# Two 64-column weight tiles in place of one 128-column tile in the experts' up projections

## The chip, the cores and the metric
The kernel runs on one core of one Trainium2 chip. The metric is the device time of one execution in microseconds (us). Three runs of the kernel before took 1402.24, 1405.08 and 1405.54 us; their median, 1405.08 us, is the number to compare with. Durations of single instructions come from one profiled execution.

## The reference, cut to what matters
The program is one inference step of a decoder layer: a mixer of a recurrent and a convolution group, a cross-attention, and a mixture of 64 experts, for 512 prompt tokens and 8 decoding tokens, all in float32. Only the experts matter here. Each token goes to 8 of 64 experts; expert e computes, for the rows x that chose it:

```
hb = jax.nn.silu(xb @ w1_e[e]) * (xb @ w3_e[e])     # (rows, 1024) @ (1024, 256), twice: the up projections
return (hb @ w2_e[e]) * g[:, None]                  # (rows, 256) @ (256, 1024), times the gate: down
```

The up projections of one expert are thus a product of 1024 input features with 512 output features (256 of w1_e, 256 of w3_e).

## The kernel before, in words
The last stage before the final sums is a loop over the 64 experts. Every expert has room for 112 rows (CAP). Five engines work on it at once, each with its own instruction order written out by hand and with semaphores between them:

- SyncE loads the three weight matrices of an expert (1 MB each) into one of four buffers in SBUF, `arena` in the profile.
- GpSimd gathers the 112 rows of x2 that the expert needs (L564), and scatters its 112 result rows (L570), both by indirect DMAs.
- TensorE does, for one expert after another, four things: `find` (5 small bfloat16 matmuls, 6 columns wide, that look up which rows belong to the expert), `turn_rows` (8 transposes of the gathered rows, L666), `up` (the up projections) and `down` (4 matmuls 512 wide). All matmuls are issued by the helper `mm` at L651, the transposes by `turn` at L666.
- ScalarE copies the transposed rows to `xgT` (L1347), takes the silu of the first half of the up result (L1351) and scales half of the down result (L1354).
- VectorE multiplies silu with the second half (L1817), scales the other half of the down result (L1820), and works out the next indices (L1803 to L1814).

In one step of TensorE's order the pieces stand as `up` of expert e, `turn_rows` of e + 1, `down` of e - 1, `find` of e + 3. So no piece needs the result of the one just ahead of it.

`up` (L1019 to L1027) holds the change. Four blocks j of 128 output features each (two of w1_e, two of w3_e) take 8 steps k of 128 input features. The weight tile, 128 x 128, is the stationary operand, the 112 gathered rows are the moving one, and the result goes to all 128 partitions of bank group 2 of PSUM, columns `at` to `at + 112`. That is 32 calls of `mm` for an expert. A call with float32 operands shows in the trace as two weight loads (LDWEIGHTS, the rows of engine PEld) and two MATMULs (engine PE), so `up` shows 64 of each. Two narrow uses of TensorE elsewhere are of interest: the router (`router`, 64 output features, at partition 0) and the transposes of decoding rows (8 partitions deep).

Of the kernel before, what the change touches and what calls it, by code (L numbers as in the profile page):

```python
# [14 lines left out]
P = 128  # L15
D = 1024
KC = D // P
# [12 lines left out]
CAP = 112  # L30
# [68 lines left out]
def decoder_step(nc: bass.Bass, ins, outs):  # L99
# [3 lines left out]
    with ExitStack() as ctx:  # L103
# [27 lines left out]
        psum = ctx.enter_context(nc.psum_tensor("psum", [P, 4, D], F32))  # L131
# [55 lines left out]
        xgT = act_mem[:, 2048:2048 + 2 * KC * CAP].rearrange("p (b k s) -> p b k s", b=2, k=KC)  # L187
# [37 lines left out]
        def value_cache(b):  # L225
            return cache(0, b) if b < 4 else cache(2, b - 4)
# [7 lines left out]
        def ew(n):  # L234

            at = 6144 * n
            return (arena[:, at:at + 4096].rearrange("p (w k n) -> p w k n", w=2, k=KC),
                    arena[:, at + 4096:at + 6144].rearrange("p (k n) -> p k n", k=2))
# [404 lines left out]
        def _(pe):  # L643
# [6 lines left out]
            def mm(out, lhsT, rhs, first, last):  # L650
                return pe.matmul(out, lhsT, rhs, start=first, stop=last)  # L651
# [12 lines left out]
            def turn(out, in_, n=P):  # L664

                return pe.transpose(out, in_, ident[0:n, 0:n])  # L666
# [3 lines left out]
            for c in range(KC):  # L670
                ps = open_group(f"x{c}")
                for t in range(TT):
                    w = width(t)
                    last = turn(ps[:, t * P:t * P + w], x_tok[0:w, t, c * P:(c + 1) * P], w)
# [38 lines left out]
            for j in range(2 * RC):  # L713
                name = ("zu", "zg")[j // RC] + str(j % RC)
                at = (j + RC) % (2 * RC)
# [3 lines left out]
            for g in range(2):  # L719
                ps = open_group(f"mt{g}")  # L720
                for c in range(4):
                    for m in range(2):
                        last = turn(ps[:, 256 * c + P * m:256 * c + P * m + P], mem_tok[:, m, (4 * g + c) * P:(4 * g + c + 1) * P])
# [20 lines left out]
            for c in range(RC):  # L744
                last = turn(ps[0:38, 512 + c * P:512 + (c + 1) * P], gluT[:, c, T - 38:T])
# [28 lines left out]
            for g in range(2):  # L774
                ps = open_group(f"kt{g}")
                for c in range(4):
                    for m in range(2):
                        last = turn(ps[:, 256 * c + P * m:256 * c + P * m + P], k_tok[:, m, (4 * g + c) * P:(4 * g + c + 1) * P])
# [3 lines left out]
            for c in range(RC):  # L782
                last = turn(ps[0:9, c * P:(c + 1) * P], ucT[:, c, SEQ - 1:T])
# [36 lines left out]
            for c in range(KC):  # L820
                last = turn(ps[0:NS, c * P:(c + 1) * P], qT[:, c, SEQ:T])
# [87 lines left out]
            for b in range(NS):  # L909
# [3 lines left out]
                for n in range(2):  # L913
                    last = mm(ps[0:NS, 512 * n:512 * n + 512], unit[:, NS * b:NS * b + NS],
                              value_cache(b)[:, 0, 512 * n:512 * n + 512], b == 0, b == NS - 1)
# [3 lines left out]
            for j in range(KC):  # L919
                last = turn(ps[:, NS * j:NS * j + NS], o_s[:, j * P:(j + 1) * P], NS)  # L920
# [41 lines left out]
            for t in range(TT):  # L962
                w = width(t)
                last = turn(ps[0:w, E * t:E * t + E], score_t[:, t * P:t * P + w], E)
# [11 lines left out]
            for t in range(TT):  # L976
                for u in range(t + 1):
                    last = mm(ps[:, E * t:E * t + E], tri if u == t else ones[:, :], sel_b[:, u, :], u == 0, u == t)
            last.then_inc(s_full, 1)
            ps = open_group("count")  # L980
            for t in range(TT):
                last = mm(ps[:, 0:E], ones[:, :], sel_b[:, t, :], t == 0, t == TT - 1)
# [36 lines left out]
            def up(b, part):  # L1019

                wu, _ = ew(part)
                for j in range(4):
                    at = 512 * b + CAP * j
                    for k in range(KC):
                        last = mm(psum[:, 2, at:at + CAP], wu[:, j // 2, k, P * (j % 2):P * (j % 2) + P], xgT[:, b, k, :],
                                  k == 0, k == KC - 1)
                return last  # L1027

            def down(b, part):
# [19 lines left out]
            def c_step(e, n, wait_w):  # L1049
                pe.wait_ge(m_xc, e + 1)  # L1050
                pe.wait_ge(s_w[n % 4], wait_w)
                if at_least(e, 2):
                    pe.wait_ge(m_hd, e - 1)
                up(n % 2, n % 4).then_inc(m_h, 1)
# [42 lines left out]
            with pe.If(n_max > CAP):  # L1097
                pe.wait_ge(m_ya, E)
                pe.wait_ge(m_yv, E)
                with pe.Fori(0, E * (ROUNDS - 1)) as i:  # L1100
                    pe.wait_ge(f_sem["oh"], i + 1)
                    find(0, i % E).then_inc(f_sem["ip"], 1)
                    pe.wait_ge(f_sem["g"], 16 * i + 16)
                    turn_rows(0).then_inc(f_sem["xt"], 1)
                    pe.wait_ge(f_sem["xc"], i + 1)
                    pe.wait_ge(f_sem["w"], 48 * i + 48)
                    up(0, 0).then_inc(f_sem["h"], 1)
                    pe.wait_ge(f_sem["hd"], i + 1)
                    down(0, 0).then_inc(f_sem["y"], 1)
# [4 lines left out]
            for n, t in enumerate(LAST_ORDER):  # L1114
# [5 lines left out]
                for q in range(3):  # L1120
                    pe.wait_ge(s_yin[q][n % 3], 16 * (n // 3 + 1))
                    for j in PE_ROWS[q]:
                        for h in range(2):
                            last = mm(psum[0:w, n % 4, 512 * h:512 * h + 512], ident[0:w, 0:w],
                                      y_in[n % 3][0:w, j, 512 * h:512 * h + 512], j == 2, j == 5)
# [836 lines left out]
```

## Time and profile before

| | |
|---|---|
| median of the three runs | 1405.08 us (1402.24 to 1405.54) |
| profiled execution, first to last instruction (the span) | 1401.5 us, 19230 instructions |
| time around the span, taken as median less span | 3.6 us |
| granted TensorE clock, mean of the span | 0.969 of full speed |
| TensorE busy: MATMUL / weight loads | 92% / 72% of the span |
| VectorE, ScalarE, GpSimd busy | 35%, 20%, 16% |
| HBM traffic | 245 GB/s over the span |

The page gives the profiled execution by its span; the runs' time is 0.7 to 4.0 us above that span, and the difference of the medians is used. In the lists "PE" is the MATMUL and "PEld" the weight load, which can run while a MATMUL runs. "128\*64 128x260" means a stationary tile of 128 rows and 64 columns with a moving operand of 128 x 260. The duration of a MATMUL or a weight load holds its way through the pipeline; what it costs in a row of its kind is the distance from one start to the next, which is read from the timeline.

### The profile page before, as it was taken

How to read it: one execution, taken by the hardware profiler on the slowest of the kernel's cores; microseconds unless marked ns; L12 is line 12 of the kernel's file. 1: busy time of each engine (PE TensorE's matmuls, PEld its weight loads, DVE VectorE, ACT ScalarE, POOL GpSimd, SP SyncE). 2: the span in 40 equal slices, each digit the busy share in tenths (PEclk: the TensorE clock that was granted, in tenths of full speed). 3: DMA queues.
4: the chain of work that ended last, by engine and by line, in shares of the span. 5: the costliest groups of instructions: out<-in, count | busy, mean ns of one | idle time of the engine just before them, and what ended most of it. 6: DMA issues, size and time to landing. Idle time of an engine off the chain costs nothing.

```text
span 1401.5 us, 19230 instructions
## 1 busy us (share of the span) xinstructions
PE 1282.4 (92%) x7579; PEld 1009.6 (72%) x7579; DVE 495.9 (35%) x1063; ACT 275.4 (20%) x454; POOL 226.2 (16%) x212
## 2 busy tenths in 40 slices
PE   5999596999979999999999999999999999999651
PEld 4888254868846685788888888888888888888420
DVE  0169998131187348111111111111111111111078
ACT  1125124022235150111111111111111111111100
POOL 2039000000000002011111111111111111111061
PEclk9999798999999999999999999999999999999887
DMA  9330303033155532688888888888888888888193
GB/s 340 152 120 2 134 11 150 1 120 136 59 190 233 181 139 69 246 312 318 321 312 313 315 313 310 306 311 308 312 314 315 312 316 311 308 309 305 41 381 160
DMA packets 75990, 319.12 MB, mean 228 GB/s; under 512 B 14055, under 2 KB 20415, under 8 KB 55941
## 3 DMA queue, kind: packets, MB, share of 16 engines
q1 hardware_dynamic: 57525, 278.60, 53.3%
q0 software_dynamic: 16992, 35.49, 7.0%
q10 hardware_dynamic: 1424, 4.35, 0.8%
q8 instruction: 34, 0.56, 0.2%
q14 instruction: 15, 0.12, 0.0%
HBM read 307.16 MB, written 36.38 MB: 245 GB/s over the span
## 4 chain that ended last, share of the span: by engine, by line
PE 77%; DVE 17%; DMA 2%; issue 1%; ACT 1%; POOL 0%; ACTq 0%; DVEq 0%; POOLq 0%; SPq 0%
PE psum L651 73%; DVE act_mem L1461 7%; PE psum L666 5%; DVE act_mem L1921 2%; DMA act_mem<-in_w_conv_b_dram 1%; DVE mk_mem L1621 1%; DVE act_mem L1529 1%; DVE st L1927 1%; DVE act_mem L1932 0%; DMA arena<-in_w_o_dram 0%; DVE act_mem L1915 0%; DVE act_mem L1559 0%; DVE act_mem L1475 0%; DMA arena<-y_rows 0%; DMA y_rows<-act_mem,idx_y 0%
## 5 line engine op out<-in xcount | busy, mean ns | idle before, releaser
L651 PE MATMUL psum<-act_mem,arena 128*128 128x112 f32 (+1 forms) x5504 | 791.6, 305 | 6.7 <-DMA arena<-in_w_o_dram 3.8
L651 PEld LDWEIGHTS psum<-act_mem,arena 128*128 128x128 f32 x5504 | 736.0, 193 | 52.6 <-DMA arena<-in_w_o_dram 4.6
L651 PE MATMUL psum<-arena,act_mem 128*112 128x512 f32 (+2 forms) x616 | 276.7, 593 | 1.0 <-DVE act_mem L1820 0.9
L651 PEld LDWEIGHTS psum<-arena,act_mem 128*112 128x112 f32 (+2 forms) x616 | 101.5, 174 | 124.5 <-issue 123.7
L570 POOL DMA_INDIRECT y_rows<-act_mem,idx_y x64 | 72.6, 1134 | 616.5 <-DVE idx_x L1814 580.4
L1817 DVE TENSOR_TENSOR act_mem<-act_mem,psum 128x224 f32<-128x224 f32 x64 | 24.8, 388 | 389.9 <-ACT act_mem L1351 389.9
L1820 DVE TENSOR_SCALAR act_mem<-psum,act_mem 112x512 f32<-112x512 f32 x64 | 48.0, 750 | 227.9 <-PE psum L651 227.9
L1351 ACT ACTIVATE act_mem<-psum 128x224 f32<-128x224 f32 x64 | 22.9, 358 | 433.3 <-PE psum L651 433.3
L1461 DVE SCALAR_TENSOR_TENSOR act_mem<-act_mem,wcb 128x511 f32<-128x511 f32 (+29 forms) x90 | 86.9, 1016 | 1.1
L1354 ACT ACTIVATE act_mem<-psum,act_mem 112x512 f32<-112x512 f32 x64 | 44.0, 687 | 164.6 <-PE psum L651 164.6
L666 PE MATMUL psum<-ident,act_mem 112*128 112x112 f32 (+4 forms) x390 | 53.5, 280 | 24.8 <-DMA act_mem<-in_x_sample_dram 10.0
L1347 ACT ACTIVATE act_mem<-psum 128x896 f32<-128x896 f32 x64 | 58.7, 917 | 60.8 <-PE psum L666 60.8
L666 PEld LDWEIGHTS psum<-ident,act_mem 112*128 112x128 f32 (+4 forms) x390 | 46.1, 179 | 30.6 <-issue 17.5
L651 PE MATMUL psum<-arena,ident 128*128 128x512 f32 x48 | 26.0, 677 | 31.4 <-DMA arena<-y_rows 31.4
L651 PEld LDWEIGHTS psum<-act_mem 128*112 128x112 bf16 x320 | 26.4, 131 | 34.7 <-issue 34.7
L1803 DVE TENSOR_TENSOR act_mem<-act_mem,gate_w 128x560 bf16<-128x560 f32 x64 | 47.3, 740 | 0.0
L526 POOL TENSOR_TENSOR act_mem<-act_mem,kv_mem 128x511 f32<-128x511 f32 (+29 forms) x30 | 44.0, 1467 | 11.4 <-ACT kv_mem L1160 9.5
L651 PEld LDWEIGHTS psum<-arena,ident 128*128 128x128 f32 x48 | 9.4, 212 | 48.0 <-issue 30.6
L651 PE MATMUL psum<-arena,kv_mem 128*128 128x512 f32 x96 | 41.8, 593 | 1.2 <-ACT kv_mem L1176 1.2
L666 PE MATMUL psum<-ident,mk_mem 112*128 112x112 f32 (+5 forms) x316 | 40.1, 269 | 1.1 <-ACT mk_mem L1314 1.1
L666 PEld LDWEIGHTS psum<-ident,mk_mem 112*128 112x128 f32 (+5 forms) x316 | 36.9, 189 | 3.3 <-ACT mk_mem L1314 2.0
L564 POOL DMA_INDIRECT act_mem<-x_rows,idx_x x32 | 32.2, 1005 | 16.3 <-issue 9.5
(221 smaller groups left out, 705.9 us busy)
## 6 DMA issues: line engine op xcount, KB each, us to landing
arena<-in_w_e_dram SPq DMA_DIRECT2D x192, 1024.0 KB, 7.9
arena<-in_w_in_dram SPq DMA_DIRECT2D x16, 512.0 KB, 16.9
arena<-in_cache_mem_k_dram SPq DMA_DIRECT2D x8, 1024.0 KB, 9.1
arena<-in_cache_mem_v_dram SPq DMA_DIRECT2D x8, 1024.0 KB, 11.6
arena<-y_rows SPq DMA_DIRECT2D x8, 1024.0 KB, 12.8
arena<-y_rows SPq DMA_DIRECT2D x4, 1536.0 KB, 8.7
arena<-in_w_v_dram SPq DMA_DIRECT2D x1, 4096.0 KB, 24.3
arena<-in_w_k_dram SPq DMA_DIRECT2D x1, 4096.0 KB, 14.0
```

The costliest lines, as they stand in the source:

```text
L526: gp.tensor_tensor(out[:, n:SEQ], out[:, n:SEQ], tap_mem[:, product % 4, 0:SEQ - n], ALU.add).then_inc(s_convp, 1)
L564: gp.indirect_dma_start(out=xg[b][0:CAP, :], out_offset=None, in_=x2_rows[:, :], in_offset=bass.IndirectOffsetOnAxis(ap=idx_x[0:CAP, n:n + ...
L570: gp.indirect_dma_start(out=y_rows[:, :], out_offset=bass.IndirectOffsetOnAxis(ap=idx_y[0:CAP, n:n + 1], axis=0), in_=ys[0:CAP, b, :], in_ ...
L651: return pe.matmul(out, lhsT, rhs, start=first, stop=last)
L666: return pe.transpose(out, in_, ident[0:n, 0:n])
L1347: return act.activation(xgT[:, b, :, :].rearrange("p (h k) s -> p h (k s)", h=2), psum[:, 1, :].rearrange("p (h n) -> p h n", h=2)[:, :, 0 ...
L1354: return act.activation(ys[0:CAP, b, 0:512], psum[0:CAP, 0, 0:512], ACT.Copy, scale=picked[0:CAP, n, 1:2])
L1461: return dve.scalar_tensor_tensor(out, in0, w, in1, ALU.mult, ALU.add)
L1803: return dve.tensor_tensor(onehot[:, n % 2, :, :], place[:, :, bass.ds(e, 1)].broadcast_to([P, TT, CAP]), numbers.unsqueeze(1).broadcast_t ...
L1817: return dve.tensor_tensor(hidT[:, b, :], silu[:, b, :], psum[:, 2, 512 * b + 2 * CAP:512 * b + 4 * CAP], ALU.mult)
L1820: return dve.tensor_scalar(ys[0:CAP, b, 512:1024], psum[0:CAP, 0, 512:1024], picked[0:CAP, n, 1:2], None, ALU.mult)
L1921: ins = dve.tensor_tensor(x, x, y_in[m % 3][0:w, j, :], ALU.add)
```

## The change
Each of the 32 calls of `mm` in `up` becomes two. The first takes the lower 64 columns of the weight tile and writes partitions 0 to 63 of the same PSUM columns, the second takes the upper 64 columns and writes partitions 64 to 127. Both have the same moving operand. Nothing else in the kernel is touched; the semaphores, the buffers and the order of the pieces stay.

```diff
                 for j in range(4):
                     at = 512 * b + CAP * j
                     for k in range(KC):
-                        last = mm(psum[:, 2, at:at + CAP], wu[:, j // 2, k, P * (j % 2):P * (j % 2) + P], xgT[:, b, k, :],
-                                  k == 0, k == KC - 1)
+                        for h in range(2):
+                            f = P * (j % 2) + 64 * h
+                            last = mm(psum[64 * h:64 * h + 64, 2, at:at + CAP], wu[:, j // 2, k, f:f + 64], xgT[:, b, k, :],
+                                      k == 0, k == KC - 1)
                 return last
```

The first place is TensorE's order where the expert loop starts: the rows "128x112" from `act_mem` and `arena` are `up`, those of L666 `turn_rows`, "112x512" is `down`, "112x6" is `find`. Before:

```order
L666 MATMUL psum<-ident,act_mem 128x112 x8
L651 MATMUL psum<-act_mem,arena 128x112 x32
L666 MATMUL psum<-ident,act_mem 128x112 x8
L651 MATMUL psum<-act_mem,arena 128x112 x32
L666 MATMUL psum<-ident,mk_mem 128x112 x8
L651 MATMUL psum<-arena,act_mem 112x512 x4
L651 MATMUL psum<-act_mem 112x6 x5
```

And the same place now:

```order
L666 MATMUL psum<-ident,act_mem 128x112 x8
L651 MATMUL psum<-act_mem,arena 64x112 x64
L666 MATMUL psum<-ident,act_mem 128x112 x8
L651 MATMUL psum<-act_mem,arena 64x112 x64
L666 MATMUL psum<-ident,mk_mem 128x112 x8
L651 MATMUL psum<-arena,act_mem 112x512 x4
L651 MATMUL psum<-act_mem 112x6 x5
```

Each `up` has 64 calls of 64 output partitions where it had 32 of 128; the pieces ahead of it and behind it, which are 112 or 128 columns wide, stand where they stood. The calls alternate between the lower and the upper partitions. The other engines' orders are the same but for line numbers.

## Rows read from the trace of the kernel before

**Rows 1.** The page: busy time of each engine, and the chain that ended last.
```profile
PE 1282.4 (92%) x7579; PEld 1009.6 (72%) x7579; DVE 495.9 (35%) x1063; ACT 275.4 (20%) x454; POOL 226.2 (16%) x212
...
PE psum L651 73%; DVE act_mem L1461 7%; PE psum L666 5%; DVE act_mem L1921 2%; DMA act_mem<-in_w_conv_b_dram 1%; DVE mk_mem L1621 1%; DVE act_mem L1529 1%; DVE st L1927 1%; DVE act_mem L1932 0%; DMA arena<-in_w_o_dram 0%; DVE act_mem L1915 0%; DVE act_mem L1559 0%; DVE act_mem L1475 0%; DMA arena<-y_rows 0%; DMA y_rows<-act_mem,idx_y 0%
```

**Rows 2.** Busy time by stretch of the expert loop; last: granted clock, DMA share, GB/s.
```profile
700.00:800.00 100.00, 100.00 (x713) 81.39 (x713) 18.16 (x49) 16.97 (x26) 17.25 (x16) 1.00 0.85 314
...
1000.00:1100.00 100.00, 100.00 (x738) 83.46 (x736) 19.62 (x53) 16.38 (x25) 19.55 (x18) 1.00 0.85 313
```

**Rows 3.** Waits of the whole span: who waited for whom, us, times, longest.
```profile
ACT act_mem L1351 <- PE psum L651: 433.3, 64, 9.1
...
DVE act_mem L1820 <- PE psum L651: 227.9, 64, 3.8
```

**Rows 4.** Groups by shape, TensorE: count, busy us, mean ns, idle before.
```profile
L651 PE MATMUL psum<-act_mem,arena 128*128 128x112 f32 x4096 | 473.7, 277 | 2.0 <-ACT act_mem L1347 2.0
...
L651 PEld LDWEIGHTS psum<-arena,kv_mem 128*128 128x128 f32 x96 | 18.2, 190 | 23.0 <-issue 21.5 <-ACT kv_mem L1176 1.4
...
L651 PEld LDWEIGHTS psum<-act_mem,gate_w 128*64 128x64 f32 x32 | 4.3, 137 | 2.8 <-issue 0.3
L651 PEld LDWEIGHTS psum<-arena,act_mem 128*8 128x8 f32 x40 | 3.3, 89 | 13.0 <-issue 12.3 <-DVE arena L1461 0.7
...
L666 PEld LDWEIGHTS psum<-ident,mk_mem 8*128 8x128 f32 x12 | 0.9, 136 | 2.4 <-ACT mk_mem L1314 2.0 <-issue 0.3
```

**Rows 5.** Timeline of one expert: start us, us, engine, line, operation, count.
```profile
807.34 0.97 PEld L666 LDWEIGHTS psum<-ident,act_mem 112*128 112x128 f32 x8
807.45 1.04 PE L666 MATMUL psum<-ident,act_mem 112*128 112x112 f32 x8
...
808.32 3.60 PE L651 MATMUL psum<-arena,act_mem 128*112 128x512 f32 x8
...
811.33 0.13 PEld L651 LDWEIGHTS psum<-act_mem 128*112 128x112 bf16 x1 [0.25 <-issue]
811.76 0.38 PE L651 MATMUL psum<-act_mem 128*112 x5
...
811.96 7.23 PEld L651 LDWEIGHTS psum<-act_mem,arena 128*128 128x128 f32 x64
811.99 7.38 PE L651 MATMUL psum<-act_mem,arena 128*128 128x112 f32 x64
...
819.10 0.97 PEld L666 LDWEIGHTS psum<-ident,mk_mem 112*128 112x128 f32 x8
```

**Rows 6.** Timeline where the router's 64-column tiles start and end.
```profile
510.02 0.38 PE L651 MATMUL psum<-act_mem,arena 128*128 128x260 f32 x1
510.33 7.23 PE L651 MATMUL psum<-act_mem,gate_w 128*64 128x260 f32 x32
...
517.18 0.38 PE L651 MATMUL psum<-act_mem,gate_w 128*64 128x260 f32 x1
517.49 0.20 PEld L666 LDWEIGHTS psum<-ident,act_mem 128*128 128x128 f32 x2 [0.39 <-ACT kv_mem L1326]
```

**Rows 7.** Timeline: eight short transposes, and short bfloat16 matmuls.
```profile
466.65 0.57 PEld L666 LDWEIGHTS psum<-ident,mk_mem 8*128 8x128 f32 x8 [2.03 <-ACT mk_mem L1314]
...
540.04 0.19 PE L651 MATMUL psum<-kv_mem,gate_w 128*128 128x64 bf16 x1
...
540.45 0.19 PE L651 MATMUL psum<-kv_mem,gate_w 128*128 128x64 bf16 x1
```

## The prediction
> **What bounds the kernel now.** I read the page's busy line and its chain first: TensorE is busy for 92% of the span, and matmuls of L651 make up 73% of the chain that ended last [rows 1]. Then the table by stretches: through the expert loop TensorE is busy without a gap, at a granted clock of 1.00 (the 2.4 GHz level), while the DMA engines are busy 0.85 of the time [rows 2]. The waits say the same from the other side: ScalarE and VectorE wait for TensorE at every one of the 64 experts [rows 3]. So in this loop every ns that TensorE needs more or less is a ns of the total, until the DMA becomes the limit. The timeline of one expert gives the prices. `up` of the next expert starts its weight loads at 811.96, the transposes behind it at 819.10: 7.14 us for 64 loads and MATMULs, or 111.6 ns for each pair [rows 5]. `find`, 0.2 us, the transposes, 0.87 us (819.10 is their start here, 807.34 that of the expert ahead), and `down`, from 808.32 to 811.76, fill the rest of a period of 11.76 us. That is 64 x 7.14 = 457 us of `up` in a span of 1401.5.
>
> The 111.6 ns are not the MATMUL's. A MATMUL 512 wide takes (811.76 - 808.32) / 8 = 430 ns from start to start [rows 5]. One 260 wide takes 219: the router's 32 run from 510.33 to 517.18, of which the first 0.05 are the exposed first weight load, so 6.80 / 31 [rows 6]. That is 0.837 ns a column and 1.3 ns besides, and so an estimated 95 ns for 112 columns. The weight load sets the pace: its duration is 89 ns for 8 columns, 137 for 64, 190 for 128 [rows 4], so 0.83 to 0.86 ns a column; 128 columns are 106.7 ns at 0.83, and 4.9 more make the 111.6 that a load takes of the load path when loads stand back to back. In step with this, the MATMUL list of `up` shows hardly any idle time before it (2.0 us over 4096) [rows 4].
>
> **The change part by part.** One call gave two loads of 128 columns and two MATMULs of 112; now the two halves give four loads of 64 columns and four MATMULs of 112, in the order lower, lower, upper, upper. Over 64 x 32 = 2048 calls:
>
> *Loads.* A 64-column load is 53.3 ns of columns and, with the same 4.9, 58.2 ns. Four make 233 ns where two made 223: +10 ns x 2048 = +20 us, if the loads go one after the other and each can start as soon as the path is free. For the fixed part the rows give bounds: the eight transposes 8 partitions deep load 128 columns at a pace of (0.57 - 0.14) / 7 = 62 ns [rows 7], where 0.14 is the duration of one [rows 4], their columns at half the price of a float32 matmul's, so 53 + 9; and the least is 1.3, as for a MATMUL. Four loads are then 218 to 249 ns, -10 to +53 us. I take 4.9, since it is the same form of load. How fast TensorE takes in instructions does not bind: fifteen short bfloat16 pairs start within 0.41 us [rows 7], under 30 ns a pair.
>
> *MATMULs.* There are four streams of 95 ns where there were two, 380 ns against 223. The trace of before has no case of two narrow tiles at different partitions. The price depends on whether a MATMUL to the upper half runs while one to the lower half does. Bound from below: the halves run beside each other, 2 x 95 = 190 ns a call (-33 x 2048 = -68 us). Bound from above: they run one after the other, 380 ns (+157 x 2048 = +321 us), more only if each change of half has to empty the array (last rival). I take them as overlapping, so that the loads, 233 ns, decide.
>
> *Entering and leaving the 64-column form.* The router shows it: the last 128-column MATMUL starts at 510.02 and streams for 217 ns, yet the first 64-column load starts only at 510.33, with no load drawn ahead; out of it the same, 517.18 to 517.49 [rows 6]. So 0.09 us of emptying at each change of form, and the next load is exposed. Before, there is no such gap: the load of `find` starts at 811.33, 0.43 ahead of its MATMUL [rows 5]. For `up` this comes at `find` -> `up`, where the 0.09 replaces about 0.02 and the first load before a MATMUL is 53 ns and not 107 (about +0.03 in all), and at `up` -> transposes: 95 ns of stream, 94 of emptying and about 55 of a load (a transpose's columns cost half), in place of 112 (+0.13). Together 0.16 us, 10 us over 64 experts; 6 if half of it is hidden, 26 if both exits pay the full 0.09 + 0.107.
>
> The other engines get the same data at the end of `up` and had been waiting [rows 3]; weights are loaded ahead in four buffers, and a longer period gives the DMA more time.
>
> *Sum.* +20 + 10 = +30 us on a span of 1401.5: 1431.5, and with the 3.6 us around the span 1435. With the bounds of both terms this case goes from 1401 to 1484.
>
> The rule that speaks against this case is about load overlap. The trace shows every float32 load starting when the MATMUL ahead of it starts, as in `down`, where the loads come 0.43 us apart like the MATMULs, and none earlier; it does not say whether a load to another half may. The Trainium skill (TensorE: Matmul & The Clock Gate, Part 3) says that weight loads overlap with MATMULs in flight only where the row group differs; here both halves use all rows. By that rule an upper load would wait for the MATMUL ahead of it, which is the third case below; without it, the sum above stands.
>
> **The rivals.**
>
> *Both halves independent, faster.* If loads to the two halves also run beside each other, the MATMUL streams decide: 190 to 200 ns a call, against 223, so -23 to -33 x 2048 = -47 to -68 us, +10 for the changes of form: 1347 to 1368, about 1357. The period of an expert falls to about 10.9 us; at a DMA share of 0.85 of 11.76 us its transfers need about 10.0, so the DMA does not stop it. For it: the emptying at the router shows that the array really takes another form for 64 columns. Against it: nothing in the trace shows two loads sharing the time; back to back they take their full 111.6. The Trainium skill (TensorEngine Tiling (Array Packing), Key Properties) says that different tiles can execute weight loads and MATMULs in parallel; no row here shows it, and by it this case would be the likeliest.
>
> *The load to the other half waits for the MATMUL ahead, slower.* Lower 1 at 0, lower 2 at 95, the upper load starts there and ends 53 later, upper 1 at about 150, upper 2 at 246, the next lower load then, lower 1 at about 301. That is 301 ns a call, +78 x 2048 = +160, +10: 1575. It decides as soon as a load may not pass a MATMUL that has not started. For it: all loads in the trace keep to this. Against it: there they all aim at the same columns, so it may only be that the place for the next weights is taken.
>
> *No overlap, slower.* 380 ns a call, +321 + 10: 1736. For it: the trace never shows two MATMULs side by side. Against it: the array changes form at the router, which would serve nothing otherwise.
>
> *Every change of half empties the array.* 95 + 94 + 53 for the MATMUL ahead of a change, 97 for the other, twice: 678 ns, +455 x 2048 = +930: 2350. This is the price of rows 6 paid 64 x 64 times; against it, that both halves are the same form.
>
> **How the numbers follow.** Loads decide: 0.38; both independent: 0.29; load waits: 0.16; no overlap: 0.12; emptying at each change: 0.05. The likeliest gives 1435, its own range 1401 to 1484. The range to hold 8 in 10 reaches from the lower end of the independent case, 1347, past the waiting load at 1575 (with its 26 us for the forms, 1591): 1347 to 1592. About 0.3% is what a measurement tells here, 1401 to 1409: that is only the lower edge of the first case, 0.04. Faster: the independent case and hardly more, 0.29. Slower: 0.67.
>
> **What would show it.** In the profile after, the distance from the first weight load of `up` to the first of the transposes: 7.5 us if the loads decide, 6.2 if the halves are independent, 9.7 if the load waits, 12.2 without overlap, over 21 with emptying. In the first case weight loads stand 58 ns apart throughout, and the first upper load of a call starts before the second lower MATMUL. The steps of 0.1 us at both ends of `up` should appear in each case. Everything outside the loop should keep its time; a lower granted clock in it, or TensorE waiting for weights, would be outside all of these.

## The result, and the profile after

The changed kernel takes 1409.25 us (median of 9 runs, 1406.46 to 1415.46) against 1402.89 us of the kernel before in the same runs (9, 1402.16 to 1406.22): a ratio of 1.0041, 95% interval 1.0026 to 1.0055. It is slower, as forecast, but by 6 us and not by 30, and mostly for reasons that the prediction does not have. The profiled span is 1411.1 us, 9.6 more than before.

The page after, busy line and the queue that brings instructions:

```profile
PE 1266.2 (90%) x11675; PEld 966.7 (69%) x11675; DVE 496.0 (35%) x1063; ACT 275.4 (20%) x454; POOL 226.8 (16%) x212
...
q8 instruction: 106, 1.74, 0.5%
```

TensorE is busy for 16 us less than in [rows 1] while the span is longer: it waits now, which it did not in [rows 2]. The second line is packets, MB and share of the DMA time; on the page before it stood as:

```profile
q8 instruction: 34, 0.56, 0.2%
```

Next, the timeline of one expert after, loads and MATMULs of `up`, GpSimd's two DMAs and the transposes behind (start us, us, engine, line, operation, count):

```profile
801.61 4.03 PEld L651 LDWEIGHTS psum<-act_mem,arena 128*64 128x64 f32 x84
801.61 4.24 PE L651 MATMUL psum<-act_mem,arena 128*64 128x112 f32 x83
...
803.17 1.19 POOL L570 DMA_INDIRECT y_rows<-act_mem,idx_y  x1 [9.06 <-DVE idx_x L1816]
804.66 1.00 POOL L564 DMA_INDIRECT mk_mem<-x_rows,idx_x  x1 [0.30 <-issue]
806.00 2.37 PE L651 MATMUL psum<-act_mem,arena 128*64 128x112 f32 x45
806.00 2.14 PEld L651 LDWEIGHTS psum<-act_mem,arena 128*64 128x64 f32 x44 [0.36 <-issue]
808.29 0.97 PEld L666 LDWEIGHTS psum<-ident,act_mem 112*128 112x128 f32 x8
```

84 loads of 64 columns start within 4.03 - 0.14 us: 47 ns from one to the next, less than the 53 ns of their columns alone. So two loads run at once, and so do two MATMULs: 83 of 95 ns each would take 7.9 us one after the other, and took 4.2. Then nothing is issued for 0.36 us. Without this gap `up` is faster still, as in the last experts, whose `up` has only the scatter beside it, no gather:

```profile
1305.03 6.14 PEld L651 LDWEIGHTS psum<-act_mem,arena 128*64 128x64 f32 x128 [0.77 <-issue]
1311.31 0.86 PEld L666 LDWEIGHTS psum<-ident,mk_mem 112*128 112x128 f32 x7
```

From the first load to the transposes it is 6.28 us, where [rows 5] have 7.14. The rest of the loss lies where TensorE's loop turns, after every eighth expert. The chain of waits around the first turn (start us, us, what):

```profile
757.05 3.65 PE psum L651 x13
760.70 2.54 issue
763.24 3.06 PE psum L651 x59
766.30 2.58 issue
768.88 1.15 PE psum L651 x11
```

"issue" is time in which TensorE waits for nothing that the profile shows. Twice in this turn it stands still for 2.5 us. The view of the loop's own line shows why (operation, count, min/median/max ns, first and last start). After, and then the kernel before:

```profile
L1090 PEldq COMPARE_BRANCH  x6: 79/5818/6197, 757.0 to 1244.4; - x6
```

```profile
L1088 PEldq COMPARE_BRANCH  x6: 76/207/240, 761.2 to 1231.6; - x6
```

The branch back takes 5.8 us and took 0.2. And the DMA queues, in the stretch from 762 to 1140 us, which begins behind the first branch back and holds three more after and four before: after, 45 packets of instructions; before, the queue does not appear in this stretch at all.

```profile
q8 instruction: 45, 0.74, 0.9%
```

The account: without stalls an expert's period, from one `up` to the next, is 11.01 us (run 9) in place of 11.76, -47 us over the 63 periods from the first `up` to the last. The gap brings the ordinary period to 11.42 (mean of 49), +25 us over 60 experts. At the five turns the two periods concerned hold 5 to 7 us more than two ordinary ones (for the first 14.04 + 5.67 + 9.88 against 2 x 11.42), 31 us in all. -47 + 25 + 31 = +9. From the start of the first `up` to that of the last the traces show +8.2 (739.5 and 747.7 us). The spans differ by 9.6, since the first `up` also starts 2.2 us later (568.1 for 565.9) and the last one takes 0.8 less.

### The profile page after: what moved, and what is told of

It reads as the page before. It is cut to its first block, busy times and chain, and to the rows that moved or that the text cites. A ratio compares the mean times of both kernels' runs of the same rounds, so it can differ in the third digit from the quotient of the medians.

```text
span 1411.1 us, 27422 instructions
## 1 busy us (share of the span) xinstructions
PE 1266.2 (90%) x11675; PEld 966.7 (69%) x11675; DVE 496.0 (35%) x1063; ACT 275.4 (20%) x454; POOL 226.8 (16%) x212
## 3 DMA queue, kind: packets, MB, share of 16 engines
q8 instruction: 106, 1.74, 0.5%
## 4 chain that ended last, share of the span: by engine, by line
PE 75%; DVE 18%; issue 4%; DMA 2%; ACT 1%; POOL 0%; ACTq 0%; DVEq 0%; POOLq 0%; SPq 0%
PE psum L651 69%; DVE act_mem L1463 7%; PE psum L666 5%; DVE act_mem L1923 2%; DVE mk_mem L1623 2%; DMA act_mem<-in_w_conv_b_dram 1%; DVE act_mem L1531 1%; DVE st L1929 0%; DVE act_mem L1934 0%; DVE act_mem L1917 0%; DVE act_mem L1561 0%; DVE act_mem L1477 0%; DMA arena<-y_rows 0%; DMA y_rows<-act_mem,idx_y 0%; DVE act_mem L1469 0%
## 5 line engine op out<-in xcount | busy, mean ns | idle before, releaser
L651 PE MATMUL psum<-act_mem,arena 128*64 128x112 f32 (+1 forms) x9600 | 749.1, 282 | 35.9 <-issue 26.5
L651 PEld LDWEIGHTS psum<-act_mem,arena 128*64 128x64 f32 (+1 forms) x9600 | 677.8, 147 | 95.2 <-issue 45.2
L666 PE MATMUL psum<-ident,act_mem 112*128 112x112 f32 (+4 forms) x390 | 60.6, 301 | 21.3 <-DMA act_mem<-in_x_sample_dram 10.5
L666 PEld LDWEIGHTS psum<-ident,act_mem 112*128 112x128 f32 (+4 forms) x390 | 48.7, 188 | 32.7 <-issue 15.6
L651 PE MATMUL psum<-arena,ident 128*128 128x512 f32 x48 | 29.1, 766 | 28.1 <-DMA arena<-y_rows 28.1
L666 PE MATMUL psum<-ident,mk_mem 112*128 112x112 f32 (+5 forms) x316 | 43.4, 280 | 3.0 <-DVE mk_mem L1623 1.9
L666 PEld LDWEIGHTS psum<-ident,mk_mem 112*128 112x128 f32 (+5 forms) x316 | 36.9, 191 | 9.9 <-issue 3.0
```

## The experiments

Theory A: the loop body of TensorE grew and is fetched again at each turn. Theory C: GpSimd's gather holds up TensorE's supply of instructions, which shows only at 24 ns an instruction. Theory H, put after run 4: it takes two of GpSimd's indirect DMAs in close succession. "Before" below is the kernel before in the same runs.

**1. A loop of 4 experts a turn.**

```diff
-            with pe.Fori(1, LAST) as i:
-                for k in range(1, NB + 1):
-                    step(NB * i + k, k, i)
+            with pe.Fori(2, 2 * LAST) as q:
+                for k in range(1, 5):
+                    e = 4 * q + k
+                    c_step(e, k % NB, 48 * (q + (k // 4 + 1)))
+                    b_step(e + 1, (k + 1) % NB, 16 * (q + ((k + 1) // 4 + 1)))
+                    y_step(e - 1, (k - 1) % NB)
+                    a_step(e + 3, (k + 3) % NB)
```

> The changed kernel, with TensorE's loop holding 4 experts in a turn where it held 8; the work and its order are the same. Theory A (the loop body no longer fits where TensorE's instructions are kept, and is fetched again at each turn): the branch at the end of a turn falls from about 5.8 us to under 0.5, the instruction queue goes from 106 packets to about 50, and the five turns give back some 31 us: 1378 us, 0.98 of the kernel before. Rival B (the stall at a turn belongs to the turn itself or to the two narrow tiles): eleven turns in place of five each keep their 6 us, and the time rises by some 35 us to 1445.

Measured: 1376.16 us, ratio 0.9798 (0.9780 to 0.9815). The branch and the instruction queue:

```profile
L1090 PEldq COMPARE_BRANCH  x12: 76/208/248, 709.8 to 1208.8; - x12
```

```profile
q8 instruction: 41, 0.67, 0.2%
```

Twelve branches of 0.2 us in place of five of 5.8, and 33 us less than the changed kernel. Theory A holds; the turn itself costs nothing. The gap in `up` stays, though the instruction queue carries no packet from 762 to 1140 us here. So the gap is not the fetch of the loop body:

```profile
1008.08 4.03 PEld L651 LDWEIGHTS psum<-act_mem,arena 128*64 128x64 f32 x84
1012.39 2.15 PEld L651 LDWEIGHTS psum<-act_mem,arena 128*64 128x64 f32 x44 [0.27 <-issue]
```

**2. The kernel before with 16 experts a turn.**

```diff
-            with pe.Fori(1, LAST) as i:
-                for k in range(1, NB + 1):
-                    step(NB * i + k, k, i)
+            with pe.Fori(0, 3) as q:
+                for k in range(1, 17):
+                    e = 16 * q + (8 + k)
...
```

> The kernel before, with its 128-column tiles, and TensorE's loop holding 16 experts in a turn where it held 8 (three turns). Theory A: the body is now larger than the one of the changed kernel, so the instruction queue stays busy through the loop (over 90 packets where there were 34) and the two branches back take about 6 us each; part of that is hidden by the matmuls that TensorE has queued, so +2 to +10 us. Rival B (the stall comes with the two narrow tiles): the branches stay at 0.2 us, the time stays within 0.3% of the kernel before.

Measured: 1409.01 us, ratio 1.0043 (1.0026 to 1.0059). Branches, instruction queue, and TensorE around the first of the two turns:

```profile
L1088 PEldq COMPARE_BRANCH  x3: 83/4245/6644, 855.0 to 1237.0; - x3
```

```profile
q8 instruction: 65, 1.06, 0.3%
```

```profile
858.50 0.38 PE L651 MATMUL psum<-act_mem 128*112 x5
861.97 4.31 PE L651 MATMUL psum<-act_mem,arena 128*128 128x112 f32 x23 [3.09 <-issue]
```

The stall needs no narrow tile, only a long body: branches of 6.6 and 4.2 us, 3.1 us of idle TensorE here. The packets were fewer than expected (65, not over 90). The Trainium skill (Runtime: NRT & Kernel Launch, Instruction fetch mechanics) gives TensorE an instruction memory of 128 KiB or 2048 instructions, refilled in blocks of 16 KiB, and says that a taken branch to a place outside its current window of two pages waits for a fetch. The trace agrees on the block: a packet of the instruction queue is 1.74 MB / 106 = 16.4 KB. An estimate by the Trainium skill's 64 bytes an instruction (128 KiB / 2048): an expert of the kernel before has 64 loads and 64 MATMULs in `up`, 42 more in the other pieces and a few that control, some 175 instructions or 11 KB, so 90 KB for eight; after it is some 300, 155 KB for eight and 78 for four; sixteen experts before are 179. By the 128 KiB the four kernels fall on the two sides as measured. By a window of two blocks the bodies of 78 and 90 KB would be fetched at each turn too, and they are not: their branches take 0.2 us, and no packet moves from 762 to 1140 us.

**3. find ahead of down, on TensorE alone.**

```diff
+                if exists(e + 3):
+                    a_step(e + 3, (k + 3) % NB)
                 y_step(e - 1, (k - 1) % NB)
-                if exists(e + 3):
-                    a_step(e + 3, (k + 3) % NB)
```

> The changed kernel, with find ahead of down in TensorE's order in place of behind it, so that find no longer stands right ahead of up; GpSimd and VectorE keep their orders, and the gather still runs during up. Theory C (the gap of 0.4 us at about the 80th pair of up comes from GpSimd's gather, which holds up TensorE's instruction supply): the gap stays, and the time stays within 5 us of 1409. Rival D (the gap comes from find standing ahead of up): the gap goes, -25 us, 1384.

Measured: 1409.77 us, ratio 1.0049 (1.0032 to 1.0065). The gap stays, mostly at pair 84 to 90; here it is inside the group of 128 loads, which takes 6.46 us and not 6.14, with both DMAs beside it:

```profile
1013.04 6.46 PEld L651 LDWEIGHTS psum<-act_mem,arena 128*64 128x64 f32 x128 [0.77 <-issue]
```

```profile
1014.81 1.19 POOL L570 DMA_INDIRECT y_rows<-act_mem,idx_y  x1 [8.94 <-DVE idx_x L1816]
1016.30 1.00 POOL L564 DMA_INDIRECT act_mem<-x_rows,idx_x  x1 [0.30 <-issue]
```

It is not `find` that makes it.

**4. The gather moved out of up.** The edit of run 3, and the same order on VectorE (`i_step` ahead of `y_step`) and GpSimd:

```diff
-                s_step(e - 1, (e - 1) % NB)
                 g_step(e + 3, (e + 3) % NB)
+                s_step(e - 1, (e - 1) % NB)
```

> The changed kernel, with find ahead of down, the indices worked out ahead of the scaling of the down result on VectorE, and the gather issued ahead of the scatter on GpSimd, so that the gather runs during down and only the scatter during up. Theory C (the gather holds up TensorE's instruction supply, which only shows when TensorE takes an instruction every 24 ns): the gap of 0.4 us goes at all of some 60 experts, -25 us, 1384, the stalls at the five turns stay. Rival E (the gap comes from any work of GpSimd or from the pace of supply alone): it stays at about the 80th pair, 1409.

Measured: 1398.94 us, ratio 0.9962 (0.9947 to 0.9976), 10 us less than the changed kernel and not 25; its runs spread from 1393 to 1403. The gap is gone from every expert; loads of two neighbours, and the MATMULs of the first:

```profile
999.93 6.14 PEld L651 LDWEIGHTS psum<-act_mem,arena 128*64 128x64 f32 x128 [0.77 <-issue]
1011.03 6.14 PEld L651 LDWEIGHTS psum<-act_mem,arena 128*64 128x64 f32 x128 [0.77 <-issue]
...
999.93 6.35 PE L651 MATMUL psum<-act_mem,arena 128*64 128x112 f32 x128
```

The period is 11.10 us and not 11.42, 19 us over 60 experts. That it is not 11.01 is probably the order's price: `down` now stands ahead of `up`, and 0.77 us pass without a load at the change of form. The five branches took longer too, 6.2 to 7.4 us; the five turns cost 36 us in this trace and 31 in that of the changed kernel.

**5. Both repairs.** The edits of runs 1 and 4 together.

> The changed kernel with both repairs: TensorE's loop of 4 experts a turn, and the gather issued during down. If the two losses are separate, the gain of the gather (61 periods of 11.10 in place of about 11.37 us, 16 us) comes off the 1376 us of the 4-expert loop: 1360 us, 0.968 of the kernel before. Rival (at a period of 11.1 us without stalls the weights' DMAs come late): TensorE waits for weights in many experts and the time stays above 1368.

Measured: 1361.88 us, ratio 0.9694 (0.9681 to 0.9708). The two losses are separate. The weights keep up in most of the six executions (1359 to 1362 us) but not in all: in the profiled one, the slowest at 1373 us, TensorE's loads waited for the weights' DMAs 12 times between 900 and 1180 us, 14.7 us in all, and the period rose to between 11.1 and 12.0 us there. The DMA engines are busy for 0.94 of that stretch, so the rival is close.

**6. The early gather in the kernel before.** The edit of run 4 with the 128-column tiles.

> The kernel before, with its 128-column tiles, and find, the indices and the gather moved forward as in the run with the early gather. If the gather only holds up the supply of instructions, and a pair every 112 ns leaves queued work enough to cover that, nothing changes: within 0.3% of the kernel before. Rival (the order itself is better): 5 us or more faster.

Measured: 1401.78 us, ratio 0.9987 (0.9978 to 0.9997), within 0.3%. At a pair every 112 ns the order does not matter. The kernel before has both DMAs during `up` too, and [rows 5] show the 64 loads beside them as one group without a gap:

```profile
813.53 1.19 POOL L570 DMA_INDIRECT y_rows<-act_mem,idx_y  x1 [9.18 <-DVE idx_x L1814]
815.02 1.00 POOL L564 DMA_INDIRECT mk_mem<-x_rows,idx_x  x1 [0.30 <-issue]
```

**7. The halves in turn, not alternating.** On run 1:

```diff
-                    for k in range(KC):
-                        for h in range(2):
+                    for h in range(2):
+                        for k in range(KC):
```

> The changed kernel with TensorE's loop of 4 experts a turn, and in up all 8 steps of the lower half of a block ahead of the 8 of its upper half (the two halves alternated call by call). Theory F (the halves overlap only because neighbours in the instruction order go to different halves; MATMULs start in order): within a run of 16 MATMULs to one half each takes 95 ns, up takes about 11.5 to 12.2 us and not 6.0, and the time goes to 1376 + 64 x 5.5 to 6.2 = 1730 to 1775 us. Rival G (each half has its own queue that runs far ahead): 1376 us, no change.

Measured: 1602.12 us, ratio 1.1411 (1.1389 to 1.1432), between the two theories. The loads of one `up`, and the transposes behind:

```profile
907.61 9.98 PEld L651 LDWEIGHTS psum<-act_mem,arena 128*64 128x64 f32 x128
917.73 0.41 PEld L666 LDWEIGHTS psum<-ident,act_mem 112*128 112x128 f32 x3
```

The loads start within 9.84 us, 1.23 for a run of 16 where 16 x 95.9 ns are 1.53 (within a run the MATMULs start 96 ns apart in the trace). So of each run some three MATMULs overlap with the next half's, no more, and alternating call by call is what makes the overlap.

**8. The gather ahead of the scatter, both during up.** On run 1, GpSimd's order swapped as in run 4.

> The changed kernel with TensorE's loop of 4 experts a turn, and on GpSimd the gather ahead of the scatter, both still during up. Theory H (any two of GpSimd's indirect DMAs in close succession use up TensorE's queued instructions): the gap comes about as long after the start of the second of them, now the scatter, and the time stays at 1376. Rival I (the gather alone does it): the gap comes some 0.93 us after the start of the gather, earlier in up, at the same length.

Measured: 1379.38 us, ratio 0.9820 (0.9804 to 0.9836). In one expert, whose `up` begins at 804.77:

```profile
806.75 1.00 POOL L564 DMA_INDIRECT mk_mem<-x_rows,idx_x  x1 [8.96 <-DVE idx_x L1820]
808.05 0.97 POOL L570 DMA_INDIRECT y_rows<-act_mem,idx_y  x1 [0.31 <-issue]
809.61 0.22 PEld L651 LDWEIGHTS psum<-act_mem,arena 128*64 128x64 f32 x4 [0.23 <-issue]
```

The gap follows the second of the two DMAs again, now the scatter, and comes at about pair 94. It begins 1.3 us after that DMA's start, where in the changed kernel it was 1.0 (from 804.66 to 805.64). Theory H holds; rival I, which had it 0.93 us after the gather, falls, and with it theory C.

**9. The gather alone during up.** On run 1, `scatter` left out on GpSimd; in its place ScalarE issues a plain DMA, of 65 rows and not 112:

```diff
                 yh(n % 2, n).then_inc(m_ya, 1)
+                act.wait_ge(m_ya, e + 1)
+                act.wait_ge(m_yv, e + 1)
+                act.dma_start(y_rows[bass.ds(65 * e, 65), :], ys[0:65, n % 2, :]).then_inc(m_s[n % 2], 16)
```

> The changed kernel with TensorE's loop of 4 experts a turn; GpSimd's indirect scatter is replaced by a plain DMA of 65 result rows to fixed rows of the same DRAM tensor, issued by ScalarE, so that the results land in the wrong rows. The gather stays in GpSimd's order, during up and behind the same wait for its indices. Theory H (GpSimd's indirect DMAs hold up TensorE's instruction supply, and it takes two of them, some 2.1 us together, to use up what is queued): with the gather alone the gap goes, up takes 6.0 us, 61 x 0.36 us = 22 us less than with the 4-expert loop, about 1355. Rival I (the gather by itself is enough): the gap stays at 0.3 to 0.45 us in up, 1376.

Measured: 1350.42 us, ratio 0.9610 (0.9588 to 0.9633). Some of the gain has nothing to do with the gap: behind the last `up` the kernel takes 84.2 us and not 88.8, 4.6 less. From the first `up` to the last it is 20.6 us less than in run 1. No gap, and from one `up` to the next 11.00 us:

```profile
1006.76 6.14 PEld L648 LDWEIGHTS psum<-act_mem,arena 128*64 128x64 f32 x128
1017.76 6.14 PEld L648 LDWEIGHTS psum<-act_mem,arena 128*64 128x64 f32 x128
```

**10. The scatter moved out of up.** On run 1, the gather ahead of the scatter, and the scatter behind the transposes:

```diff
                 gp.wait_ge(m_yv, e + 1)
+                gp.wait_ge(m_xt, min(e + 4, E) if isinstance(e, int) else e + 4)
```

> The changed kernel with TensorE's loop of 4 experts a turn, and with GpSimd's gather ahead of its scatter, the scatter waiting until the transposes behind up are done, so that only the gather is issued during up and the scatter during down; TensorE's order is that of the changed kernel. Theory H (two indirect DMAs during up use up TensorE's queued instructions, one does not): no gap, a period of 11.01 us as with the plain scatter, 22 us less than the 1376 us of the 4-expert loop: 1354, some 7 us under the version with the early gather (period 11.10). Rival J (the later scatter is waited for by the scaling of the next down result, whose buffer it reads): the period grows again, 1365 or more.

Measured: 1356.34 us, ratio 0.9660 (0.9644 to 0.9675), the fastest version that computes the whole reference, 3.4% under the kernel before and 3.8% under the changed one. The scatter runs during `down`, the gather during `up`:

```profile
802.62 3.60 PE L652 MATMUL psum<-arena,act_mem 128*112 128x512 f32 x8
...
803.71 0.97 POOL L570 DMA_INDIRECT y_rows<-act_mem,idx_y  x1 [5.44 <-PE psum L667]
...
806.36 5.76 PEld L652 LDWEIGHTS psum<-act_mem,arena 128*64 128x64 f32 x120
...
808.38 1.00 POOL L564 DMA_INDIRECT act_mem<-x_rows,idx_x  x1 [3.70 <-DVE idx_x L1821]
```

## Why the prediction was wrong

**The loads, +20 us: wrong.** "If the loads go one after the other": they do not. Two loads to different halves run side by side, and the MATMUL streams decide: in run 4, 128 MATMULs start within 6.09 us (6.35 less the 0.26 of the last one), 48 ns from one to the next or 192 ns a call, where the forecast had 233 and the rival of independent halves 190 to 200. This was the term that was mis-sized, by 41 ns x 2048 = 84 us. The kernel before had loads to one and the same place only, so its rows could not show it; they bounded it, and the range held the result, but I gave the independent case 0.29. The Trainium skill (TensorEngine Tiling (Array Packing), Key Properties), which has different tiles load and multiply in parallel, was right here: 47 ns from load to load. The Trainium skill's other rule (TensorE: Matmul & The Clock Gate, Part 3), loads beside running MATMULs only where the row group differs, does not hold for these halves, which use all rows.

**The change of form: right in kind, too small.** Gapless, `up` takes 6.28 us to the transposes, 6.2 forecast for this case. But the period fell by 0.75 us (11.76 to 11.01), and 32 calls at 192 ns in place of 223 are 1.00 us. So the changes of form cost 0.25 us an expert and not 0.16, 16 us over 64 where 10 were forecast, within the bounds of 6 to 26. The emptying is as forecast: from the last MATMUL to the transposes' first load it is 0.19 us in run 9, 95 ns of it stream.

**The supply of instructions: the step that failed.** "How fast TensorE takes in instructions does not bind", I wrote, from fifteen pairs within 0.41 us [rows 7]. That is a burst of 30 instructions; it says nothing of a body that has to be fetched, nor of a stream of 256 instructions at 24 ns each with other work beside it. The pace itself can be kept: `up` has no gap in runs 4, 9 and 10. Doubling the calls cost two things here. The body of the loop outgrew the place where it was kept, 33 us by run 1 against the changed kernel. And TensorE stood idle behind GpSimd's two indirect DMAs, 20 us by run 10 against run 1 and 21 by the loop of run 9; that its queued instructions ran out there is my reading, since the gap shows only at the faster pace. Neither loss was among the rivals, so the independent case at 1357 had the stage right and the total wrong: it is what runs 5, 9 and 10 measure, 1350 to 1362.

**The sign: right by chance.** 30 us were forecast as loads plus changes of form; what was measured of these two is a gain of 47 us, and two losses of 56 that were not in the sum turned it into a small loss.

**Outside the loop**: the time behind it stayed, as said (89.0 us behind the last `up`, before and after). Ahead of it the 2.2 us are no effect of the change: with the same code there, the first `up` starts at 565.1 us in run 10 and at 569.6 in run 4. The granted clock did not stay at 1.00 in the loop: the stretches of 100 us with a turn show 0.98, since TensorE falls to its lower level (0.50, 1.2 GHz, at 861.5 us) after stops of 2.5 us and more; the sum above has that in the turns.

What stays open: by which path GpSimd's indirect DMAs hold up TensorE. Runs 3, 4, 8, 9 and 10 show that the gap goes with their number and place; none shows the mechanism, and two of them further apart within one `up` were not tried. The exact size at which a loop body no longer stays lies between the eight experts of the kernel before and the eight of the changed one.

## What to carry to other kernels

Where short MATMULs wait for weight loads, two 64-column tiles that alternate call by call run side by side and took a float32 call from 223 to 192 ns; it doubles the instructions, so count them first: the packets of the instruction queue within a loop should be zero, and a branch back of several us is a body that is too long. Then look at what else shares the supply: here one of GpSimd's two indirect DMAs was better issued while TensorE had long MATMULs queued. When a step makes an engine's instructions twice as many, a short burst in the trace is no evidence that they can be delivered.

## What the runs showed of the hardware that I had not expected

- Weight loads and MATMULs of two 64-column float32 tiles overlap fully when they alternate (two MATMULs in 96 ns, what one takes alone in run 7), and by only some three MATMULs of a run of 16 when they come in turn (run 7).
- A branch back of TensorE's loop takes 0.2 us with the body kept and 4.2 to 7.4 us with a body that has to be fetched (runs 1, 2 and 4), with 128-column tiles too (run 2).
- Two indirect DMAs of GpSimd in succession, 2.2 us together, leave TensorE idle for 0.2 to 0.5 us when it takes an instruction every 24 ns; one alone does not (runs 4, 9 and 10), and at one every 56 ns two do not either (the kernel before, and run 6 against it).
